# Rows of keys and values turned by VectorE in 32x32 blocks instead of by TensorE, in a one-core decoder step

## The reference

```python
h = rmsnorm(x, g_pre) * (1 + scale) + shift
q, k, v, z_a, z_b, xbc, dt, r_a, r_b = split(h @ w_in)      # q, k, v: 3 groups x 8 heads x 128
for window, d in ((128, 1), (512, 4), (2048, 16)):           # dilated attention
    o, lse = attend(q, k, v, window, d)
    new_buffer = stack([k, v])[:, -min(window, 512):]        # an output: rows by token
o_a = combine(o, lse) * silu(z_a)
y_b = ssd(conv(xbc), dt) ...                                 # Mamba-2 branch
out = (sigmoid(r_a) * (o_a @ w_o_a) + sigmoid(r_b) * (y_b @ w_o_b)) @ w_o
y = x + gate * rmsnorm(out, g_post)
```

## Time and profile before

| | |
|---|---|
| median of the runs | 2959.39 us (3 runs, 2959.34 to 2968.88) |
| span of the profiled execution | 2959.8 us |
| TensorE, busy | 2895.4 us, 98% |
| VectorE, ScalarE, GpSimd, busy | 1919.4, 901.6, 1236.4 us |
| granted TensorE clock | 0.998 of full |
| HBM read, written | 630.85, 245.17 MB |

### The profile page before, as it was taken

One profiled execution on the slowest core, in us unless ns is written; L12 is line 12 of the kernel. 1 busy time (PEld: TensorE's weight loads), 2 busy tenths in 40 slices (PEclk: granted clock), 3 DMA queues, 4 the chain that ended last, 5 costly groups with the idle time before them and its releaser, 6 DMA issues.

```text
span 2959.8 us, 51731 instructions
## 1 busy us (share of the span) xinstructions
PE 2895.4 (98%) x22132; PEld 2780.8 (94%) x22132; DVE 1919.4 (65%) x2114; ACT 901.6 (30%) x1459; POOL 1236.4 (42%) x583
## 2 busy tenths in 40 slices
PE   6999999999999999999999999999999999999998
PEld 4898899999999999999999999999999989999886
DVE  3303788898885888979886767787777865212302
ACT  3122122333233233333322233343433343212322
POOL 1133344444443444444454545444544534444432
PEclk9999999999999999999999999999999999999999
DMA  9879886654356876656657666666657665876643
GB/s 345 338 271 356 308 296 241 219 209 144 136 164 208 292 290 238 225 210 249 253 219 267 238 238 218 213 234 241 206 208 243 225 218 195 308 261 231 251 178 142
DMA packets 221035, 704.82 MB, mean 238 GB/s; under 512 B 26932, under 2 KB 130604, under 8 KB 171372
## 3 DMA queue, kind: packets, MB, share of 16 engines
q1 hardware_dynamic: 158262, 471.33, 45.5%
q0 software_dynamic: 5248, 174.60, 14.5%
q10 hardware_dynamic: 57296, 55.59, 5.6%
HBM read 630.85 MB, written 245.17 MB: 296 GB/s over the span
## 4 chain that ended last, share of the span: by engine, by line
PE 83%; DVE 9%; DMA 6%; issue 2%; POOL 1%; ACT 0%; SPq 0%; DVEq 0%; ACTq 0%; POOLq 0%
PE acc L1460 22%; PE acc L1462 22%; PE acc L1461 22%; DMA side<-in_keys_t 3%; DVE side L1889 1%; DMA w_raw<-in_w_ada_t 1%; PE ps_s L1329 1%; DVE side L2260 1%; DVE side L2126 1%; DMA side<-in_w_ada_t 1%; DVE side L2257 1%; DVE side L2262 1%; PE ps_s L1589 1%; PE ps_t L1474 1%; PE ps_s L1709 1%
## 5 line engine op out<-in xcount | busy, mean ns | idle before, releaser
L936 POOL TENSOR_TENSOR w_lo<-w_raw,w_hi 128x1024 fp32r<-128x1024 f32 (+1 forms) x416 | 1096.0, 2653 | 1680.9 <-ACT w_hi L995 1680.9
L1460 PE MATMUL acc<-act,w_hi 128*128 128x288 f32 x5744 | 1715.1, 299 | 3.0 <-POOL w_lo L936 2.8
L1462 PE MATMUL acc<-act,w_lo 128*128 128x288 f32 x5744 | 1692.2, 295 | 0.0
L1461 PE MATMUL acc<-act,w_hi 128*128 128x288 f32 x5744 | 1692.0, 295 | 0.0
L1460 PEld LDWEIGHTS acc<-act,w_hi 128*128 128x128 f32 x5744 | 1078.4, 188 | 23.8 <-issue 12.4
L1461 PEld LDWEIGHTS acc<-act,w_hi 128*128 128x128 f32 x5744 | 1078.6, 188 | 1.9
L1462 PEld LDWEIGHTS acc<-act,w_lo 128*128 128x128 f32 x5744 | 1078.0, 188 | 0.0
L995 ACT ACTIVATE w_hi<-w_raw 128x1024 fp32r<-128x1024 f32 (+1 forms) x418 | 404.0, 1015 | 478.2 <-PE acc L1462 190.2
L1918 DVE TENSOR_TENSOR side<-side 128x2048 f32<-128x2048 f32 x96 | 273.3, 2847 | 81.7 <-DMA side<-in_vals_t 67.1
L1889 DVE TENSOR_TENSOR side<-side 128x2048 f32<-128x2048 f32 x96 | 263.6, 2746 | 86.2 <-DMA side<-in_keys_t 82.6
L1070 ACT ACTIVATE ev<-acc 128x576 f32<-128x576 f32 x112 | 72.9, 651 | 604.1 <-PE acc L1462 603.0
(11 more groups left out here) (363 smaller groups left out, 2806.2 us busy)
## 6 DMA issues: line engine op xcount, KB each, us to landing
w_raw<-in_w_in_t SPq DMA_DIRECT2D x160, 1024.0 KB, 7.8
out_s_kv<-in_cache_a_w POOLq DMA_DIRECT2D x80, 1632.0 KB, 9.0
side<-in_keys_t SPq DMA_DIRECT2D x52, 1024.0 KB, 8.2
side<-in_vals_t SPq DMA_DIRECT2D x52, 1024.0 KB, 8.0
out_s_kv<-in_cache_a_w POOLq DMA_DIRECT2D x24, 1344.0 KB, 8.3
w_raw<-in_w_ada_t SPq DMA_DIRECT2D x24, 1024.0 KB, 8.7
w_raw<-in_w_gate_t SPq DMA_DIRECT2D x16, 1024.0 KB, 10.6
w_raw<-in_w_o_b_t SPq DMA_DIRECT2D x16, 1024.0 KB, 7.5
```

Of the source, the lines that this page charges most:

```text
L936: nc.gpsimd.tensor_tensor(dst, raw[:, SLOT[s], ks, 0:cols], wh[:, u % 2, ks, 0:cols].bitcast(F32), ALU.subtract).then_inc(lo, 1)
L1460: nc.tensor.matmul(out, wh[:, c, k, 0:cols], high, start=(k == 0), stop=False)
L1461: nc.tensor.matmul(out, wh[:, c, k, 0:cols], low, start=False, stop=False)
L1462: mm = nc.tensor.matmul(out, wl[:, c, k, 0:cols], high, start=False, stop=(k == kt - 1))
```

## The change

TensorE's `token_rows`, ScalarE's copy and their semaphores go. VectorE gets `turn_rows`: one 32x32 block transpose of the 128x512 tile out of `ev` into a free part of `raw` (`blocks`, two buffers), at the end of its list in the odd half of the next unit, after the grains and attention. Partition 32a + j then holds, for each of 16 blocks of 32 tokens, the 32 features of block a of token j of that block. ScalarE stores this with four DMAs per destination, one for each 32 partitions, in runs of 128 bytes in place of 512; a v unit has two destinations. `store_rows` moves behind `store_samples`, ahead of attention in the odd half. There are two semaphores for landed stores, one for each buffer. SyncE's load of the value rows moves two halves later. ScalarE's `store_unit` waits for the turn before it overwrites `ev`.

```diff
-HEAD_DMAS = [{"k": 1, "v": 2}.get(kind, 0) for kind in KINDS]
+HEAD_DMAS = [{"k": 4, "v": 8}.get(kind, 0) for kind in KINDS]
...
+        blocks = raw[:, 2, 0:8, :].rearrange("p (a k) n -> p a (k n)", a=2)
...
-                    if j == 4 * PACE * h:
-                        sp.wait_ge(tok_out, HEAD_OUT[HEADS0 + 7 * h + 5])
+                    if j == 4 * PACE * h + 2:
+                        for c in range(2):
+                            sp.wait_ge(tok_out[c], HEAD_OUT[c][HEADS0 + 7 * h + 5])
...
                 if g == 0 and i:
                     sp.wait_ge(lo, 2 * ENTRY[THIRD_LAST][1] + 2)
+                    for c in range(2):
+                        sp.wait_ge(tok_out[c], HEAD_OUT[c][NU - 1])
...
-                act_e.wait_ge(tok_t, n + 1)
-                if n:
-                    act_e.wait_ge(tok_out, HEAD_OUT[u - 1])
-                nc.scalar.activation(tokst[:, 0:4, :], ps_t[:, :].rearrange("p (t e) -> p t e", e=E), ACT.Copy).then_inc(tok_c, 1)
-                act_e.wait_ge(tok_c, n + 1)
-                t0 = 3 if gi == 0 else 0
-                order = "(p t) e -> p t e" if BY_CLASS[u] else "(t p) e -> p t e"
-                act_e.dma_start(outp[gi][:, "qkv".index(kind) - 1, h, :].rearrange(order, p=P), tokst[:, t0:4, :]).then_inc(tok_out, 16)
+                act_e.wait_ge(tok_b, n + 1)
+                first = 12 if gi == 0 else 0
+                outputs = [(outp[gi][:, "qkv".index(kind) - 1, h, :], first)]
                 if kind == "v":
-                    cols = slice(gi * AW + h * E, gi * AW + (h + 1) * E)
-                    act_e.dma_start(S["kvtok"][:, cols].rearrange("(t p) e -> p t e", p=P), tokst[:, 0:4, :]).then_inc(tok_out, 16)
+                    outputs.append((S["kvtok"][:, gi * AW + h * E:gi * AW + (h + 1) * E], 0))
+                for dst, b0 in outputs:
+                    for a in range(4):
+                        rows = slice(32 * a, 32 * a + 32)
+                        act_e.dma_start(dst[:, rows].rearrange("(b j) e -> j b e", j=32),
+                                        blocks[rows, n % 2, 32 * b0:SEQ].rearrange("p (b e) -> p b e", e=32)).then_inc(tok_out[n % 2], 16)
...
+                if v in HEAD_ROWS:
+                    act_e.wait_ge(tok_b, HEAD_ROWS.index(v) + 1)
...
-                if u and u - 1 in HEAD_ROWS:
-                    store_rows(u - 1)
...
                 if u and u - 1 in LAST_ROWS:
                     store_samples(u - 1)
+                if u and u - 1 in HEAD_ROWS:
+                    store_rows(u - 1)
                 attention(2 * u + 1)
...
-            def token_rows(u):
-
-                n = HEAD_ROWS.index(u)
-                pe.wait_ge(evac, EVACS[u])
-                pe.wait_ge(smp_c, sum(1 for v in LAST_ROWS if v < u))
-                for t in range(4):
-                    mm = nc.tensor.transpose(ps_t[:, t * P:(t + 1) * P], ev[:, u % 2, t * P:(t + 1) * P], ident[:, :])
-                mm.then_inc(tok_t, 1)
-
             def sample_rows(u):
...
-                if u in HEAD_ROWS:
-                    pe.wait_ge(tok_c, HEAD_ROWS.index(u) + 1)
...
-                if u and u - 1 in HEAD_ROWS:
-                    token_rows(u - 1)
...
+            def turn_rows(u):
+
+                n = HEAD_ROWS.index(u)
+                dve.wait_ge(evac, EVACS[u])
+                if n == 0:
+                    dve.wait_ge(lo, 2 * ENTRY[THIRD_LAST][1] + 2)
+                if n >= 2:
+                    dve.wait_ge(tok_out[n % 2], HEAD_OUT[n % 2][HEAD_ROWS[n - 2]])
+                src = ev[:, u % 2, 0:SEQ]
+                if BY_CLASS[u]:
+                    src = src.rearrange("p (r i) -> p i r", r=4)
+                nc.vector.transpose(blocks[:, n % 2, :], src).then_inc(tok_b, 1)
...
+                if half % 2 and u and u - 1 in HEAD_ROWS:
+                    turn_rows(u - 1)
```

More of the change, by code:

```diff
@@ L195 @@
 LAST_ROWS = [u for u, kind in enumerate(KINDS) if kind in "qkv"]
-HEAD_DMAS = [{"k": 1, "v": 2}.get(kind, 0) for kind in KINDS]
+HEAD_DMAS = [{"k": 4, "v": 8}.get(kind, 0) for kind in KINDS]
 LAST_DMAS = [{"q": 1, "k": 2, "v": 2}.get(kind, 0) for kind in KINDS]
-HEAD_OUT = [16 * sum(HEAD_DMAS[:u + 1]) for u in range(NU)]
+HEAD_OUT = [[16 * sum(HEAD_DMAS[v] for v in HEAD_ROWS[c::2] if v <= u) for u in range(NU)] for c in range(2)]
 LAST_OUT = [16 * sum(LAST_DMAS[:u + 1]) for u in range(NU)]
@@ L476, in phase_all @@
         stored = sems("stored0", "stored1")
-        tok_t, tok_c, tok_out = sems("tok_t", "tok_c", "tok_out")
+        tok_b, tok_out = m.sem("tok_b"), sems("tok_out0", "tok_out1")
         smp_t, smp_c, smp_out = sems("smp_t", "smp_c", "smp_out")
@@ L1307, in _ @@
                         squares(group, t)
-            act_e.wait_ge(tok_out, HEAD_OUT[NU - 1])
+            for c in range(2):
+                act_e.wait_ge(tok_out[c], HEAD_OUT[c][NU - 1])
             act_e.wait_ge(smp_out, LAST_OUT[NU - 1])
```

## The result

The changed kernel takes 3022.11 us (median of 4 runs, 3019.75 to 3025.52) against 2959.36 us (4 runs); the ratio is 1.0203, with an interval of 1.0188 to 1.0218. It is slower by 63 us; the forecast was 2966 (2937 to 2995). Lines of the changed kernel: matmuls L1466 to L1468, scores of the prompt attention L1503 to L1505, transposes of the exp L1511, exp L1097, ScalarE's copy of the turned scores L1106, evacuation L1075 and L1072, high weights L999, low weights L940, last scaling L2050, the turn L2370, its stores L1013.

A forecast was written before the change was run, and what follows sets the result against it. TensorE, busy 98% of 2959.8 us, was taken as the bound. 2959.8 less 21.1 for removed transposes plus 28 of waits for the exp gave 2966.7, forecast as 2966 us, range 2937 to 2995.

The forecast's parts named there:

- Removed work: On TensorE, 48 groups of four transposes go, 0.44 us each, 21.1 us in all.
- The turn: On VectorE, 48 block transposes of 128x512 are added at 0.65 us each, 31 us against 134 us idle in the stretch.
- D: Time ScalarE spends issuing a unit's row stores: 4.0 to 6.5 us for a value unit, 2.0 to 3.2 for a key unit.
- The third rival: ScalarE's queue doesn't take eight DMAs in a row; at 1 us an issue the time is 2990 us; chance 0.18.
- Where these fall: Turn wait and issues ahead of attention in ScalarE's order delay the exp; TensorE loses 18.9 to 37.8 us, middle 28.
- The forecast's own formula: Each attention step loses 1.19 + D, plus 1.28 us table load after a z unit, less TensorE's slack behind the exp.
- does a stall heal itself?: No: late ScalarE delays weight split and SyncE's key and value loads, so VectorE is late again and step losses add up.
- D + 0.84: TensorE's loss at the attention step at 544.49, after a value unit: 4.8 to 7.3 us.
- DMA engines: 122,880 pieces of 128 bytes replace 30,720 of 512; 46 us more over 820, 6%, taken at no cost in time.
- The fourth rival: A 128-byte store costs two 512-byte ones, so decode values land 60 us late and the time is 2998; chance 0.10.
- The rule of the Trainium skill: For DMA stores, line rate begins at 512 B and less goes through a read-modify-write; by it the sum would be 2998.
- The moved loads of the value rows: SyncE's loads wait for stores two halves (13.8 us) later; cost nothing, or up to 2 us without the stall.

## Why the prediction was wrong

**Removed work: right.** 21.1 us forecast, 21.0 measured in the stage, 18 in the whole.

**The turn: right for 32 of 48.** They took 0.70 us for the forecast 0.65. The 16 turns of keys by class, which read a strided source, took 1.1 us, such as this one:

```profile
501.32 1.09 DVE L2370 STREAM_TRANSPOSE w_raw<-ev 128x512 f32<-128x512 f32 x1
```

All 48 together are 40 us of VectorE where 31 were forecast.

**D: above its high case for values.** 7.2 us on average, and 4.0 to 11.6 from unit to unit, where 4.0 to 6.5 was used; 2.8 for keys where 2.0 to 3.2 was. The third rival, that held issues make it slower, decided "from a D of about 6.3 us": it had the sign and the place, with a chance of 0.18, and its 2990 was 32 us short. Its own sign, most issues at 1 us and more, was not seen: the median stayed at 0.50 to 0.53 us.

**Where these fall: the step that failed.** Per step, forecast and measured:

| step before | loss forecast | measured at L1511 | measured at L1503 |
|---|---|---|---|
| 544.49 | 4.8 to 7.3 | 16.41 at 559.65 | |
| 603.74 | 2.2 to 3.4 | 2.66 at 619.88 | |
| 951.59 | 6.4 to 8.9 | 1.41 at 989.23 | 11.45 at 970.56 |
| 1155.15 | 3.0 to 5.5 | 4.59 at 1214.50 | 1.99 at 1195.37 |
| the other steps | 2.5 to 12.7 | 17.2 | 6.5 |
| sum | 18.9 to 37.8 | 42.3 | 19.9 |

What failed here: D was taken as 4.0 to 6.5 us at every value unit, the exp as the only operation behind it on which TensorE waits, and the first step's VectorE as no later than before. The term that was mis-sized most is D. The forecast's own formula, with the slack of before and the D that was measured at each step (4.3 to 11.6 us for values, 1.8 to 2.4 for keys), gives about 60 us where 18.9 to 37.8 stood. At L1511 42.3 were measured: more at the first step, and less at later value steps, where VectorE stood further ahead of TensorE than before. At 989.23, behind TensorE's loss at 970.56, its last scaling had ended 11.3 us before TensorE arrived, where it was 1.2 before. Of the four steps the working holds with its parts at 619.88 alone (D 2.0, scaling 1.6 us ahead for 2.1). At 1214.50 D was 10.0 and the scaling 8.5 us ahead for 4.6: two errors cancel there, and the 4.59 us fall into the range by luck. In the same way the 60 us of the formula are near the 62.2 of the stage only by chance, as the formula lacks two things.

First, turn and issues stand in every odd half under which rows are stored, also in that two halves after the exp, where the copy L1106 is queued behind them; the text named the copy and then counted only the exp. At 970.56 this was 11.45 us, in the timelines of VectorE and ScalarE:

```profile
949.43 2.29 DVE L1911 TENSOR_TENSOR side<-side 128x2048 f32<-128x2048 f32 x1 [16.87 <-ACT side L1123]
...
960.74 0.70 DVE L2370 STREAM_TRANSPOSE w_raw<-ev 128x512 f32<-128x512 f32 x1
```

```profile
961.47 2.82 ACTq L1013 DMA_DIRECT2D out_p_kv<-w_raw  x4
964.33 5.49 ACTq L1013 DMA_DIRECT2D kvtok<-w_raw  x4
969.91 0.60 ACT L1106 ACTIVATE side<-ps_s 128x512 f32<-128x512 f32 x1 [18.03 <-issue]
```

VectorE came late to that turn because its value grain waited for ScalarE's softmax of the samples (L1123), which stood behind a unit's issues in the half before. Most of this wait is old; in VectorE's timeline of the kernel before it is

```profile
925.71 2.29 DVE L1918 TENSOR_TENSOR side<-side 128x2048 f32<-128x2048 f32 x1 [12.33 <-ACT side L1118]
```

but there the copy didn't wait for VectorE. So this loss could have been read from the trace of before.

Second, the first step was reckoned from VectorE's times of before. But the stores start at 472.07, some 70 us ahead of it, and what they delay had come round by then. The forecast's D + 0.84 gives 8.0 of the 16.4 us with the measured D of 7.2. The other 8.4 us are VectorE's lateness: 6.1 us behind TensorE in place of 2.7 ahead of it, less the 0.44 that TensorE gained. The question "does a stall heal itself?" was answered with no, by the road of SyncE's loads, with VectorE late again at the next step. That road is seen ahead of the first step. At the 24 later steps of the stage it is not: VectorE's last scaling ended 1.6 to 11.3 us before TensorE arrived, at one of them 2.7 us less than in the kernel before, at the others at most 0.7 less or even more. The losses add up all the same, since TensorE has no idle time in which to win them back. A chunk of keys or values takes no longer from issue to landing (7.5 and 7.7 us, 8.2 and 8.0 before); it is issued later.

**The clock: not in the sum.** Behind the first stall, in TensorE's timeline, starts are 0.24 us apart at first and 0.13 from 562.94 on:

```profile
560.60 0.44 PE L1467 MATMUL acc<-act,w_hi 128*128 128x288 f32 x1
560.84 0.44 PE L1468 MATMUL acc<-act,w_lo 128*128 128x288 f32 x1
...
562.94 0.30 PE L1468 MATMUL acc<-act,w_lo 128*128 128x288 f32 x1
563.08 0.30 PE L1466 MATMUL acc<-act,w_hi 128*128 128x288 f32 x1
```

Busy time multiplied by what the granted clock lacked, summed over stretches of 2 us from 440 to 1300, is 15.1 us, against none before.

**The sum again.** For the stage: -21.1 + 62.2 - 1.9 + 15.1 = +54.3, measured +58.1. 3.8 us are not assigned.

**DMA engines: right.** The stores' queue, in the page of the changed kernel:

```profile
q10 hardware_dynamic: 152912, 55.60, 7.2%
```

Before it had 57,296 packets and 5.6%. By the trace's packet records the 95,616 more packets took 3472 - 2672 = 800 us of engine time, 50 us of 16 engines; 46 were forecast. A piece of 128 bytes took 13.1 ns, one of 512 in the kernel before 27.9; 12.6 and 26.4 were used. The fourth rival is refuted: it took a 128-byte store to cost as much as two long ones. The rule of the Trainium skill weighed there (DMA: Bandwidth & Descriptors, section Specifications) therefore did not decide; the trace agrees with it that bytes per time fall. The moved loads of the value rows cost nothing, as forecast: no wait of TensorE in the stage stands ahead of the products with the values.

Settled by runs that change one cause: the late turn and the many issues cost little alone (7.0 and 8.3 us, each at the edge of the noise) and 79 together. Not settled: what holds a single issue for 6 us. That the first step's lateness comes round through the weights and SyncE's loads was read from the timelines; its share of the 79 us was not isolated. Issuing the stores from another engine's queue was not tried.

## What to carry to other kernels

When an engine's queue also issues DMAs, an issue that waits for another engine is a stop sign for everything behind it: put what it waits for early in the other engine's list. Moving this one turn from the end to the head of its half was worth 71 us, as much as one issue per destination (72), which leaves the order of the rows out; and the resulting kernel (2951.3) is 0.4% faster than the one before. Don't price eight issues in a row by the median of single ones. When a slack is counted at one consumer, count it for each operation queued behind the new wait, and ask how late its producer already is when the first consumer comes.

## What was not expected of the hardware

The cost of several DMA issues in a row is not a constant of their number: the same eight issues of a value unit took 7.2 us with the late turn and 5.4 with the early one (longest single issue 6.0 and 3.6 us). In the changed kernel none of the 48 first issues of a unit took over 0.45 us, and 38 of the 40 issues over 1 us began with three or more of the queue's earlier stores not yet landed; in the kernel with runs of 512 bytes there were as many issues and only 11 over 1 us. That is a coincidence in time and no cause shown.

VectorE's small last scaling (128x2) took 0.214 us in the median before and 0.854 in the changed kernel (0.170 with the turn first). All 20 of the changed kernel's 32 that took over 0.3 us end with a GpSimd operation that began earlier, as in these rows of VectorE and GpSimd:

```profile
929.78 2.17 DVE L2050 TENSOR_SCALAR small<-lse 128x2 f32<-128x2 f32 x1
```

```profile
927.18 4.75 POOL L940 TENSOR_TENSOR w_lo<-w_raw,w_hi 128x1024 fp32r<-128x1024 f32 x2 [8.38 <-ACT w_hi L999]
```

Both end at 931.9. The Trainium skill (SBUF — State Buffer, section Who interferes with whom) has the two engines share a pair of ports, which the first to issue keeps for its whole instruction where VectorE's operation wants it too; the trace agrees here. At this place GpSimd's low weights, which follow ScalarE's high weights (L999), ran into VectorE's last scaling; whether the late evacuations brought this about was not tried.
